# Modulation weights split by ScalarE and GpSimd, five groups beside the preparation, two attention units at once in block 1

## The reference

```python
proj = rmsnorm(h) @ w_in
q, k, v, u = split(proj)                       # 16 query heads, 4 key heads of 64; u has 1024 channels
attn = sliding_window_attention(rmsnorm(q), rmsnorm(k), v, sinks)
ssm  = s5_mixer(u, lam, log_step, b, c, d, w_glu, b_glu)   # diagonal complex state space model
h = h + concat(rmsnorm(attn), rmsnorm(ssm)) @ w_out
h = h + square(relu(rmsnorm(h) @ w_up)) @ w_down
```

```python
mod   = silu(c)     @ w_ada + b_ada            # w_ada is 2048 x 12288
mod_c = silu(c_ctx) @ w_ada + b_ada
```

## Time and profile before

| what | value |
|---|---|
| time, median of 3 runs | 4931.92 us (4926.59 to 4939.75) |
| time of the profiled execution | 4934.87 us |
| its span in the profile | 4933.4 us |
| projection ends, `heads` begins | about 161 us from the span's start |
| `heads` and `states` | up to 223.2 us |
| the four turns of `mixers1` | 223.2 to 868.0 us |
| TensorE busy over the span | 87% |

### The profile page before, as it was taken

One profiled execution on the slowest core, in us unless ns is written; L12 is line 12 of the kernel. 1 busy time (PEld: TensorE's weight loads), 2 busy tenths in 40 slices (PEclk: granted clock), 3 DMA queues, 4 the chain that ended last, 5 costly groups with the idle time before them and its releaser, 6 DMA issues.

```text
span 4933.4 us, 69710 instructions
## 1 busy us (share of the span) xinstructions
PE 4316.6 (87%) x28096; PEld 3667.4 (74%) x28096; DVE 2810.2 (57%) x5619; ACT 1548.4 (31%) x2683; POOL 0.2 (0%) x4
## 2 busy tenths in 40 slices
PE   7598899699999989999877778777778897999997
PEld 7333223689999978889767777777645797999997
DVE  4756444566556542234557777777632476655654
ACT  3211111444444432234122222222100243444442
POOL 0000000000000000000000000000000000000000
PEclk9799999899999999999789899998989999999999
DMA  5344555346565654457451112121422463655653
GB/s 174 96 147 147 169 163 155 121 153 190 187 187 180 192 149 120 115 147 208 120 150 51 55 52 58 50 58 40 127 70 75 156 200 116 192 187 185 186 188 112
DMA packets 383056, 669.52 MB, mean 136 GB/s; under 512 B 43897, under 2 KB 77402, under 8 KB 382220
## 3 DMA queue, kind: packets, MB, share of 16 engines
q1 hardware_dynamic: 327168, 595.74, 40.2%
q10 hardware_dynamic: 55564, 69.31, 4.3%
HBM read 634.87 MB, written 29.46 MB: 135 GB/s over the span
## 4 chain that ended last, share of the span: by engine, by line
PE 63%; DVE 13%; issue 2%; ACT 2%; DMA 1%; ACTq 0%; DVEq 0%
PE acc L547 13%; PE acc L549 12%; PE acc L548 12%; PE acc L589 8%; PE bank L548 2%; PE bank L547 2%; PE bank L549 2%; PE bank L1654 2%; PE bank L1663 2%; PE bank L1661 1%; ACT weights_hi L511 1%; PE bank L2130 1%; DVE arena L1493 1%; PE acc L1462 1%; PE bank L734 1%
## 5 line engine op out<-in xcount | busy, mean ns | idle before, releaser
L526 DVE TENSOR_TENSOR weights_lo<-weights_ring,weights_hi 128x512 fp32r<-128x512 f32 x1600 | 1094.1, 691 | 1022.5 <-ACT weights_hi L511 1020.9
L511 ACT ACTIVATE weights_hi<-weights_ring 128x512 fp32r<-128x512 f32 x1600 | 994.3, 630 | 1078.8 <-PE acc L549 882.3
L548 PE MATMUL acc<-arena_halves,weights_hi 128*128 128x256 f32 (+2 forms) x3136 | 916.3, 292 | 0.0
L547 PE MATMUL acc<-arena_halves,weights_lo 128*128 128x256 f32 (+1 forms) x2944 | 860.4, 292 | 21.7 <-DVE weights_lo L526 12.2
L549 PE MATMUL acc<-arena_halves,weights_hi 128*128 128x256 f32 (+1 forms) x2944 | 858.8, 292 | 0.0
L547 PE MATMUL acc<-moving_halves,weights_lo 128*128 128x256 f32 (+1 forms) x2816 | 792.1, 281 | 73.0 <-DVE weights_lo L526 72.3
L549 PE MATMUL acc<-moving_halves,weights_hi 128*128 128x256 f32 (+1 forms) x2816 | 786.6, 279 | 0.0
L548 PE MATMUL acc<-moving_halves,weights_hi 128*128 128x256 f32 x2624 | 731.4, 279 | 0.0
L548 PEld LDWEIGHTS acc<-arena_halves,weights_hi 128*128 128x128 f32 x3136 | 590.5, 188 | 12.1
L547 PEld LDWEIGHTS acc<-moving_halves,weights_lo 128*128 128x128 f32 x2816 | 535.7, 190 | 81.6 <-DVE weights_lo L526 53.6
L589 PE MATMUL acc<-moving,weights_ring 128*128 128x256 f32 x2304 | 581.2, 398 | 10.4 <-ACT arena L692 9.3
(11 more groups left out here) (422 smaller groups left out, 4830.9 us busy)
## 6 DMA issues: line engine op xcount, KB each, us to landing
weights_ring<-in_w_in SPq DMA_DIRECT2D x624, 256.0 KB, 2.7
weights_ring<-in_w_ff SPq DMA_DIRECT2D x512, 256.0 KB, 3.0
weights_ring<-in_w_ada SPq DMA_DIRECT2D x384, 256.0 KB, 2.9
weights_ring<-in_w_up SPq DMA_DIRECT2D x256, 256.0 KB, 2.9
weights_ring<-in_w_down SPq DMA_DIRECT2D x256, 256.0 KB, 3.2
weights_ring<-in_w_out SPq DMA_DIRECT2D x128, 256.0 KB, 3.2
weights_ring<-in_w_branch SPq DMA_DIRECT2D x96, 256.0 KB, 3.3
s_state<-arena ACTq DMA_DIRECT2D x36, 256.0 KB, 2.8
```

The costliest lines, as they stand in the source:

```text
L511: a.activation(whi, k.slot(g.ring0 + kc), ACT.Copy).then_inc(*s.made("scalar_done", "high", n))
L526: v.tensor_tensor(wlo, k.slot(g.ring0 + kc), whi.bitcast(F32), ALU.subtract).then_inc(*s.made("vector_done", "low", n))
L547: pe.matmul(g.out[m], wlo[:, cols], xhi, start=first, stop=False, skip_group_check=g.shared)
L548: pe.matmul(g.out[m], whi[:, cols], xlo, start=False, stop=False, skip_group_check=g.shared)
```

## The change

It has these parts.

1. `cc` is split into halves too: `cc4` holds for each chunk the high halves of the two vectors and the low halves, four stationary columns. All `w_ada` sums have four rows now; the rows are written, read back and added (two more loads, two more transposes, two more additions before block 2).
2. The first `WHOLE_ADA = 5` groups stay whole (true fp32). They are handed out beside `heads` and `states`, which now stand in lockstep with each other.
3. The other 19 groups (304 chunks) are split: ScalarE writes `weights_hi`, GpSimd writes `weights_lo` and frees the slot of the ring, TensorE runs two fp32r matmuls for each chunk, `BEHIND = 3` pieces later. They use the same five halves' buffers in turn.
4. `attention` becomes two strands, one for each half of the queries, beside one strand of all eight channels: 129 rounds, with `pieces` 137.
5. Even and odd groups of `w_ada` have an accumulator bank of their own.
6. `qk_sq` and `qk_rs` lie elsewhere, so that `heads` and `states` can run at once.

```diff
-def mixers1(k, attention, channels, modulation):
-    for turn in range(NKV):
-        beside(lockstep([attention(k, turn), pair_of(channels, k, turn)]), 56,
-               [(modulation(k, k.groups["w_ada", 6 * turn + n]), 17) for n in range(6)])
+def mixers1(k, me, heads, states, whole, attention, channels, split):
+
+    beside(lockstep([heads(k), states(k)]), 19, [(whole(k, k.groups["w_ada", n]), 17) for n in range(WHOLE_ADA)])
+    barrier(k, me, "heads")
+    beside(lockstep([attention(k, 0), attention(k, 1), all_channels(channels, k)]), 137,
+           [(split(k), len(split_modulation(k)) + 2 * BEHIND)])
+    barrier(k, me, "mixers1")
...
-def attention_vector(k, kv):
+def attention_vector(k, b):
...
-    for u in range(8):
-        n, hh, qt, b = 8 * kv + u, u // 2, u % 2, u % 2
+    for n in range(b, 32, 2):
+        kv, hh, qt = n // 8, n % 8 // 2, b
...
+def split_modulation_scalar(k):
+    a, s, chunks = k.nc.scalar, k.s, split_modulation(k)
+    for i in range(len(chunks) + 2 * BEHIND):
+        if i < len(chunks):
+            g, kc = chunks[i]
+            n, whi, wlo = halves(k, g, kc)
+            a.wait_ge(*s.at("weights", g.ring0 + kc))
+            if n >= k.HALVES:
+                a.wait_ge(*s.at("halves_used", n - k.HALVES))
+            a.activation(whi, k.slot(g.ring0 + kc), ACT.Copy).then_inc(*s.made("scalar_done", "high", n))
+        if i >= 2 * BEHIND and chunks[i - 2 * BEHIND][1] == KD - 1:
+            modulation_row(k, chunks[i - 2 * BEHIND][0])
+        yield
+
+def split_modulation_gpsimd(k):
+    p, s = k.nc.gpsimd, k.s
+    for g, kc in split_modulation(k):
+        n, whi, wlo = halves(k, g, kc)
+        p.wait_ge(*s.at("high", n))
+        p.tensor_tensor(wlo, k.slot(g.ring0 + kc), whi.bitcast(F32), ALU.subtract).then_inc(*s.made("gpsimd_done", "low", n))
+        s.mark("gpsimd_done", "ring_free", g.ring0 + kc)
+
+def split_modulation_tensor(k):
+    pe, s, chunks = k.nc.tensor, k.s, split_modulation(k)
+    for i in range(len(chunks) + 2 * BEHIND):
+        if BEHIND <= i < len(chunks) + BEHIND:
+            g, kc = chunks[i - BEHIND]
...
+            pe.wait_ge(*s.at("low", n))
+            pe.matmul(g.out[0], k.cc4[:, kc, :], wlo, start=kc == 0, stop=False)
+            pe.matmul(g.out[0], k.cc4[:, kc, :], whi, start=False, stop=kc == g.kchunks - 1).then_inc(
+                *s.made("tensor_done", "halves_used", n))
```

More of the change, by code:

```diff
@@ L319, in places @@
         self.lp1, self.lp2 = a.take(8 * (P + 16)), a.take(8 * (P + 16))
+        self.qk_sq, self.qk_rs = (b.take(10, L) for b in (self.space(a.at), self.space(a.at + 10 * L)))
         self.w, self.cs, self.sn = a.take(8, L), a.take(8, L), a.take(8, L)
@@ L809, in heads_scalar @@
     s.mark("kdup", "kdup")
+    for _ in range(8):
+        yield
 def heads_tensor(k):
@@ L825, in heads_tensor @@
             *s.made("tensor_done", "qk_sum", c))
+        if c % 2:
+            yield
+    for _ in range(10):
+        yield
 def heads_vector(k):
@@ L913, in attention_vector, with attention_scalar @@
         yield
[L915 removed]
+def attention_scalar(k, b):
     a, s = k.nc.scalar, k.s
[L917 to L918 removed]
+    for n in range(b, 32, 2):
+        kv, hh = n // 8, n % 8 // 2
         head, sc = 4 * kv + hh, k.att_s[:, b, :]
@@ L942, in states_scalar, with states_tensor @@
     a.activation(t3, k.turns, ACT.Sin, scale=TWO_PI_BELOW / 2).then_inc(*s.made("scalar_done", "turn_sines"))
+    for _ in range(5):
+        yield
+def states_tensor(k):
+    for _ in range(8):
+        yield
 def states_vector(k):
@@ new lines, in split_modulation_vector, with modulation_gpsimd, all_channels @@
+def split_modulation_vector(k):
+    for _ in range(len(split_modulation(k)) + 2 * BEHIND):
+        yield
+def modulation_gpsimd(k):
+    split_modulation_gpsimd(k)
+def all_channels(channels, k):
+    for c in range(8):
+        yield from channels(k, c)
+def mixers1(k, me, heads, states, whole, attention, channels, split):
[4 more added lines that the diff above has]
+    barrier(k, me, "mixers1")
@@ L1158, in output1_scalar @@
     a.wait_ge(*s.at("mods_out", 23))
-    rows = k.mix[0:96, 0:2, 0:P]
-    for r in range(2):
+    rows = k.mix[0:96, 0:4, 0:P]
+    for r in range(4):
         a.dma_start(rows[:, r, :], k.io["s_mods"][r:r + 1, :].rearrange("a (c p) -> (a c) p", p=P)).then_inc(*s.landed("mods_in"))
@@ L1206, in output1_vector @@
         serial(k, v.tensor_tensor(k.mods[:, :, r], k.bank[r][:, 0:96], k.p("b_ada"), ALU.add))
+    for r in range(2):
+        v.wait_ge(*s.at("mods_t", r + 2))
+        serial(k, v.tensor_tensor(k.mods[:, :, r], k.mods[:, :, r], k.bank[r + 2][:, 0:96], ALU.add))
     for c in (16, 64):
```

105 lines of the change are left out of this document (65 added, 40 removed).

## The result

The changed kernel takes 4987.38 us (median of four runs, 4985.40 to 4989.86); the kernel before took 4932.24 us in four runs beside it. The ratio is 1.0101, with a 95% interval of 1.0086 to 1.0117: one per cent slower. The forecast was 4872 and its range ended at 4970. The profiled execution took 4989.86 us, its span 4988.4.

A forecast was written before the change was run, and what follows sets the result against it. The prediction took TensorE's modulation to set the turns. From 4934.9 us it replaced 644.8 of turns by a 566 us main stage and added 14 for preparation and 2 for ends: 4872 us, range 4775 to 4970.

The forecast's parts named there:

- Both at SBUF: Main stage: 23 VectorE operations a channel wait 0.43 us each on GpSimd subtractions, 9.8 us a channel, 78 in all.
- the waiting term: Main stage: VectorE's waiting for GpSimd subtractions at SBUF, with GpSimd busy 0.7 of the time, 78 us.
- The tail: End of the main stage, after the last output matmuls: 14 chunks at GpSimd's 1.22 us, 17 us.
- waiting for drive matmuls: Channels of the main stage: half of VectorE's 6.6 us wait a channel goes, 3.3 us, as background between them shrinks.
- the base: Main stage without SBUF waiting: six channels of 63.5 us, two of 45.0, and a tail of 17.
- row loads: Ahead of the context: two more loads at 0.4 us each, with two transposes and two small additions, 2 us.
- The sign of a blocked VectorE: Main stage: the scan grows from 724 ns or shows idle time before it; operations with one PSUM operand don't.
- those for a wrong forecast: Subtraction over 1.5 us, TensorE waiting for `weights_lo` all stage, preparation over 85 us, or main-stage clock at half.
- No conflict: Main stage: GpSimd and VectorE don't hinder each other at SBUF, 78 us less, 4794 us; chance 0.25.
- GpSimd wins nearly every time: Main stage: VectorE's listed operations wait for whole subtractions, 19.7 to 28.1 us a channel, 4951 to 5018 us; chance 0.18.
- GpSimd is the bound: Main stage: 304 subtractions set its length, gain gone from 2.07 us each, 5324 us at 3.35; chance 0.15 with coupling.
- The coupled rival: Main stage: buffers couple four engines so tightly that a channel takes 80 us, 4963 us; chance 0.15 with GpSimd as bound.

The follow-up runs named there:

- e1_narrow: The changed kernel, but GpSimd subtracts one column in 512, all instructions and waits kept: 4814.45 us, 0.9763 of the kernel before.
- e5_fill: The changed kernel with three write-only GpSimd fills of the low half in place of each subtraction: 4929.30 us, 0.9977 of the kernel before.
- m1_alone: A separate kernel without the computation: ten kinds of VectorE operation alone, then beside GpSimd subtractions; the scan went from 0.75 to 1.27 us.
- e2_whole: The changed kernel with all 24 groups whole in true fp32, without ScalarE's and GpSimd's part in them: 4828.57 us, 0.9792 of the kernel before.

## Why the prediction was wrong

**The step that failed** is "Both at SBUF": "23 a channel ... 0.43 × 23 = 9.8 us a channel, 78 in all". The list was too short; the price of what it had came out. From the groups of the change less those of e1_narrow:

| operations | a channel | extra in all | for one |
|---|---|---|---|
| counted: L1069, L1070, L1081, L1084, L1086, L1096, L1098, L1101, L1103 | 23 | 77 us | 0.42 us |
| not counted: L1078, L626, L1105, and L926 and L930 of attention | 20 | 92 us | 0.57 us |

The counted ones came to 77 us where 78 were taken. The second row is the error. The prediction's own words were "two operands in SBUF, or at double rate", but the list under them took only the longest operation of the second kind (L1037, now L1081), and left out L1078's eight short ones, the copies and scales (L626, L1105, L930), and attention's whole share, four units a channel. What a blocked operation pays is the rest of a subtraction, whatever its own length: L926 pays 0.83 us on 0.15.

That 78 met 77 so closely is partly luck. The prediction let each operation meet a subtraction at random, with a chance of 0.7 and 0.61 us left of it. By the start times in the trace 111 of the 184 counted ones (0.60) began while a subtraction ran, and paid 0.69 us each. It wasn't at random: L1084 and L1086 never met one and L1081 once in eight. GpSimd has no converted chunk there, since ScalarE stands at the sines in its program and waits for L1084 (57.1 us in all). Of the 160 others 100 began during a subtraction (0.62, hardly more often), but they paid 0.92 us each. L1078 began 0.16 us into the running subtraction on average and L926 and L930 0.28, where the counted L1096 began 0.91 us into it.

The section that the prediction named (the Trainium skill, "SBUF — State Buffer", "Who interferes with whom") lists `tensor_scalar` and copies, under conditions, beside the operations with two SBUF inputs, says that two-input ones contend only with a GpSimd instruction that reads SBUF, and that reductions never contend on this chip. The trace and runs agree: beside fills the scan kept 725 ns and L1078 went to 601 (e5_fill), and the reduction kept 0.47 us beside subtractions (m1_alone).

**The other terms.** The second stage begins at 240.6 us, 237 forecast. The sum had left two waits at nothing: TensorE stood 1.8 us for weights from HBM (its weight loads 8.8), and 0.9 us at the end for ScalarE's copy of the last row. The clock was full, as counted. Chunks cost 0.86 us whole and 0.46 as a pair at the start of the tail (granted clock 1.00), as taken. The subtraction, taken at 1.22 us, measures 1.24 when alone. The estimate of 1.12 us from the Trainium skill's figure ("GPSIMD Engine Reference", "Elementwise — side-by-side cycle accounting") is lower. It would have moved the sum by more than the 1 or 2 us that the prediction names: the waiting term goes by the subtraction's length twice (share of the time that GpSimd is busy, and what is left of one), and 78 us become 66. The tail took 19.6 us for 17. Without a conflict the stage was put at 488 us and e1_narrow shows 504: its first six channel periods are 64.4 us for 63.5, but the last two 51.9 and 51.6 for 45.0. That term was too small by 13 us. Of the 6.6 us a channel of waiting for drive matmuls half was to go, and in these two it was 7.6; the wait for the sixteen output matmuls (L1109) was 9.1 us a channel, where it had been 6.3. The 364 chunks that the prediction takes off TensorE's 566 us are 378 by the starts in the trace; nothing in the sum hangs on them.

**The sum again.** The stage took 117 us more than forecast: 16 for the base, 88 for blocked operations (166 less 78), 11 for VectorE's idle time, and 2 left over. With 3 us more of preparation, and 3 less behind the stage (2 us of row loads were forecast there, and 0.8 came off, within what that stretch varies by between profiled runs), that is the miss of 118 on the profiled execution.

**The signs named beforehand.** The sign of a blocked VectorE came: the scan grew and L1093, with an operand in PSUM, didn't. Of those for a wrong forecast one came: the subtraction lasts 1.50 us on average, against 1.24 alone, because VectorE blocks it too. Another came in part: TensorE waits 161.8 us for `weights_lo` in the stage. Most of that is slack of an engine that isn't the bound, as VectorE's 11 us of added idle time show. Channel periods are 85.7 us for six and 73.4 for two, where near 73 and 55 were named.

**The rivals.** "No conflict" was worth 4794 by the sum and 4814 by e1_narrow: near, for a kernel that nobody can use. "GpSimd wins nearly every time" (4951 to 5018) holds the result, and its break-even, 141 us of waiting over the stage, was passed at 166; but its mechanism isn't what happened to the 23 operations it was worked out for, which paid 0.42 us each and not 0.86 or 1.22. GpSimd is the bound in no run: it is busy 447 of 681 us in the change, and 478 of 619 in e5_fill, where the coupling through the five buffers did show. The coupled rival named 80 us a channel and 4963; the periods passed 80, but e1_narrow, with the same buffers and waits, has 64.4. What the forecast itself lacked was the question that e2_whole asks: not whether the split makes TensorE lighter (it did, 383 us in e1_narrow against 482 in e2_whole), but whether TensorE would still be the bound once two units run at once.

**Open.** The granted clock in the stage is 0.76 in the change, 0.84 in e1_narrow and 0.96 in e2_whole. Whether that costs the change time by itself, no run isolates. VectorE's idle time, where waiting for a slower TensorE would show, grew by only 11 us over e1_narrow. Why attention's and L1078's operations begin so early in a subtraction wasn't tried.

## What to carry to other kernels

Before you hand element-wise work to GpSimd, list every operation that VectorE runs beside it with two operands in SBUF, the one-column ones too, and every scale or copy of several columns from SBUF to SBUF. Charge each with a third to half of a GpSimd operation (0.42 to 0.57 us here at 1.24 us an operation, GpSimd busy two thirds of the time): 344 of them made VectorE 166 us busier, for work that cost it 181 to do itself. Look for such a loss in mean durations against the kernel before, not in the waits. And when one edit gives the engines more independent work to overlap (two units at once, modulation beside the preparation) and another makes the bound engine lighter (the split), try the first alone: here it held the whole gain.

## What the runs showed of the hardware

- A VectorE sum of one column takes 0.15 us alone and up to 1.23 beside GpSimd's subtractions (mean 0.975 over 32). A reciprocal of one column kept its 0.16 us, although 24 of 32 began during a subtraction.
- A scan that begins during a subtraction lasts longer by what is left of that subtraction less 0.14 us (42 scans of the change).
- A GpSimd that only fills memory leaves VectorE's scans and sums untouched (725 and 442 ns) and still stretches scales from SBUF to SBUF, 350 to 601 ns. A fill of 128x512 fp32 takes about 0.52 us on GpSimd, a subtraction 1.24.
- The block works both ways: GpSimd's subtraction is 1.25 us at least, 1.50 on average in the stage.
- Beside the preparation the weight loads moved 319 GB/s over 16.8 us, at a DMA share of 0.95. TensorE waited 1.8 us for them in 80 chunks (and its weight loads 8.8), so at 0.86 us a chunk of 256 KB, 305 GB/s, the queue was about even with TensorE.
